# When raw weight slots are given back, and two accumulators for layer 0's modulation

## The reference, cut to what matters

```python
def modulation(cond, w_mod, b_mod):
    m = jax.nn.silu(cond) @ w_mod + b_mod
    return jnp.split(m[:, None, :], 6, axis=-1)

for li in range(DEPTH):
    sh1, sc1, g1, sh2, sc2, g2 = modulation(cond, w_mod[li], b_mod[li])
    h = x * (1 + sc1) + sh1
    ...                                   # the mixer: h @ w_in, then its own work, then @ w_out
    x = layer_norm(ALPHA * x + g1 * out, ln_g[li, 0], ln_b[li, 0])
    h = x * (1 + sc2) + sh2
    x = layer_norm(ALPHA * x + g2 * moe(h, ...), ln_g[li, 1], ln_b[li, 1])
```

## Time and profile before

| | |
|---|---|
| three runs, median | 2907.91 us (2905.69 to 2911.71) |
| the profiled execution, first to last instruction | 2919.7 us |
| TensorE busy with matmuls | 2612.8 us, 89% |
| VectorE, GpSimd, ScalarE busy | 1430.2, 797.6, 752.2 us |
| weights and all else read | 517.73 MB, 179 GB/s over the span |

### The profile page before, as it was taken

The page is one execution under the profiler, slowest core; times in us unless marked ns, Lnnn a source line. Parts: engine busy times, 40 slices in busy tenths (PEclk is TensorE's granted clock), DMA queues, the critical chain, the costliest instruction groups (busy, mean ns, idle before and its releaser), DMA issues.

```text
span 2919.7 us, 30216 instructions
## 1 busy us (share of the span) xinstructions
PE 2612.8 (89%) x11960; PEld 1918.1 (66%) x11960; DVE 1430.2 (49%) x1955; ACT 752.2 (26%) x1263; POOL 797.6 (27%) x429
## 2 busy tenths in 40 slices
PE   5779899998898998899998877789999899989997
PEld 3778864445896787744458866676444699864444
DVE  6456553334645676633336389974333415650013
ACT  1132130002454451300013344432001334230111
POOL 3355400001363344000014478830000247500000
PEclk8789889998699998899999878898999899979999
DMA  7443639893241216388944411054989143528881
GB/s 265 168 124 101 193 143 334 321 360 110 76 137 37 73 58 180 137 326 316 362 162 138 143 48 37 24 183 150 332 324 348 51 135 101 149 99 300 301 297 41
DMA packets 291851, 524.41 MB, mean 180 GB/s; under 512 B 9472, under 2 KB 141056, under 8 KB 291328
## 3 DMA queue, kind: packets, MB, share of 16 engines
q1 hardware_dynamic: 288256, 519.33, 51.4%
q10 hardware_dynamic: 3456, 3.15, 0.3%
HBM read 517.73 MB, written 4.72 MB: 179 GB/s over the span
## 4 chain that ended last, share of the span: by engine, by line
PE 75%; DVE 12%; ACT 4%; DMA 3%; issue 3%; POOL 2%; SPq 0%; ACTq 0%; DVEq 0%
PE ps L1877 23%; PE ps L1892 11%; PE ps L1625 6%; PE ps L1626 6%; PE ps L1627 6%; PE ps L1690 3%; DVE macc L1964 2%; POOL wlo L1557 2%; DVE uw L1318 2%; PE ps L1648 1%; PE ps L1816 1%; PE ps L1650 1%; PE ps L1649 1%; PE ps L1840 1%; PE ps L1841 1%
## 5 line engine op out<-in xcount | busy, mean ns | idle before, releaser
L1557 POOL TENSOR_TENSOR wlo<-ring,whi 128x1024 fp32r<-128x1024 f32 x202 | 533.6, 2657 | 1514.3 <-ACT whi L1424 1514.3
L1877 PE MATMUL ps<-ring,xg 128*128 128x512 f32 x1536 | 708.0, 606 | 0.0
L1877 PEld LDWEIGHTS ps<-ring,xg 128*128 128x128 f32 x1536 | 290.5, 194 | 329.6 <-issue 329.2
L1964 DVE SCALAR_TENSOR_TENSOR macc<-ring,cond_s,macc 128x1024 f32<-128x1024 f32 x322 | 438.9, 1424 | 10.6 <-DMA ring<-w_mod 10.6
L2182 DVE SCALAR_TENSOR_TENSOR hid<-ps,cws,sg 128x256 f32<-128x256 f32 x96 | 46.4, 484 | 674.6 <-ACT sg L1518 674.6
L1892 PE MATMUL ps<-ring,hidt 128*128 128x512 f32 x768 | 349.9, 599 | 2.3 <-ACT hidt L1493 2.3
L1625 PE MATMUL ps<-hh,whi 128*128 128x384 f32 x832 | 303.4, 365 | 27.3 <-POOL wlo L1557 21.0
L1626 PE MATMUL ps<-hl,whi 128*128 128x384 f32 x832 | 291.0, 350 | 0.0
L1627 PE MATMUL ps<-hh,wlo 128*128 128x384 f32 x832 | 290.9, 350 | 0.0
L1424 ACT ACTIVATE whi<-ring 128x1024 fp32r<-128x1024 f32 x202 | 207.2, 1055 | 307.4 <-DMA ring<-gmlp_w_out 115.2
L1892 PEld LDWEIGHTS ps<-ring,hidt 128*128 128x128 f32 x768 | 147.4, 193 | 187.4 <-issue 187.4
(11 more groups left out here) (361 smaller groups left out, 4112.3 us busy)
## 6 DMA issues: line engine op xcount, KB each, us to landing
ring<-moe_w_gu SPq DMA_DIRECT2D x192, 1024.0 KB, 7.5
ring<-w_mod SPq DMA_DIRECT2D x96, 1024.0 KB, 8.2
ring<-moe_w_down SPq DMA_DIRECT2D x96, 1024.0 KB, 5.1
ring<-gmlp_w_in SPq DMA_DIRECT2D x32, 1024.0 KB, 5.7
ring<-ssd_w_in SPq DMA_DIRECT2D x21, 1024.0 KB, 5.3
ring<-hgrn_w_in SPq DMA_DIRECT2D x20, 1024.0 KB, 5.2
ring<-gmlp_w_out SPq DMA_DIRECT2D x16, 1024.0 KB, 5.7
ring<-ssd_w_out SPq DMA_DIRECT2D x8, 1024.0 KB, 6.0
```

Of the source, the lines that this page charges most:

```text
L1557: pool.tensor_tensor(split_sub(wlo, s0), raw_sub(s0), split_sub(whi, s0).bitcast(F32), ALU.subtract).then_inc(S["lo_ready"], 1)
L1877: ins = pe.matmul(ps[:, s % 2, :], xg[:, w, k, :], whole(what, s, 4)[:, k % 4, :], start=(k == 0), stop=(k == KD - 1))
L1964: ins = dve.scalar_tensor_tensor(out=macc[:, v, :], in0=w[:, k, :], scalar=by, in1=macc[:, v, :], op0=ALU.mult, op1=ALU.add)
```

## The change

A slot that held a mixer chunk is given back when GpSimd has written the low part of its second half (`lo_ready`), and not when TensorE has finished it (`sub_done`). Raw weights are read by ScalarE and GpSimd alone, so nothing reads the slot after that. The counts in the wait are the same.

Groups 2 and 4 of layer 0 add into a second accumulator, `macc_b`, which lies where the gated MLP's `gsh` comes to lie later. The first chunk of a group waits for the sum of the last group before it that used the same accumulator and was not done by TensorE alone, in place of the group just before it. The other groups and layers stay on `macc`.

```diff
@@ -57,6 +57,7 @@
 PE_GROUPS = (1,)
+B_GROUPS = (2, 4)
@@ -242,6 +243,7 @@
         macc = ar("macc", [P, 2, D], F32, 76)
+        macc_b = ar("macc_b", [P, 2, D], F32, 24)
@@ -379,7 +381,7 @@
                 elif chunk_rows[p] > 0:
-                    sp.wait_ge(S["sub_done"], nth[2 * p] + 2)
+                    sp.wait_ge(S["lo_ready"], nth[2 * p] + 2)
@@ -513,6 +515,10 @@
+        def acc_of(group):
+
+            return macc_b if group in B_GROUPS else macc
@@ -1687,7 +1693,7 @@
-                    ins = pe.matmul(ps[:, 7, c:c + 1], macc[:, v, j * P:(j + 1) * P], ones[:, 0:1], start=True, stop=True)
+                    ins = pe.matmul(ps[:, 7, c:c + 1], acc_of(group)[:, v, j * P:(j + 1) * P], ones[:, 0:1], start=True, stop=True)
@@ -1953,15 +1959,19 @@
                 elif q == 0:
-                    dve.wait_ge(S["mod_summed"], m // MOD_GROUP)
+                    group = m // MOD_GROUP
+                    held = max((g for g in range(group) if acc_of(g) is acc_of(group) and g not in PE_GROUPS), default=None)
+                    if held is not None:
+                        dve.wait_ge(S["mod_summed"], held + 1)
+                acc = acc_of(m // MOD_GROUP)
...
-                            ins = dve.tensor_scalar(macc[:, v, :], w[:, k, :], by, None, ALU.mult)
+                            ins = dve.tensor_scalar(acc[:, v, :], w[:, k, :], by, None, ALU.mult)
...
-                            ins = dve.scalar_tensor_tensor(out=macc[:, v, :], in0=w[:, k, :], scalar=by, in1=macc[:, v, :],
+                            ins = dve.scalar_tensor_tensor(out=acc[:, v, :], in0=w[:, k, :], scalar=by, in1=acc[:, v, :],
```

## The result

The changed kernel takes 2928.6 us in the median of 12 runs (2916.7 to 2932.3), the kernel before 2910.6 us beside it; the ratio is 1.0051, with a 95% interval of 1.0038 to 1.0064. One of the 12 runs of before, in a slow state, took 3431.7 us and does not enter the ratio. I had forecast 6.1 us and a range up to 2920.5. The direction was right, the size was not. The profiled execution of the changed kernel spans 2922.9 us, only 3.2 us more than that of before: that of the changed kernel lay 4 us under its median, that of before about 11 above.

The account below looks back on a forecast made before the run. It took TensorE, three quarters of the chain that ended last, to bound the kernel. Terms of 0 + 0.4 + 4.6 + 3.2 - 2.1 = +6.1 us on 2907.9 gave 2914.0 us, range 2902.5 to 2920.5.

Parts of the forecast that it names:

- the two out-part terms: Out parts of layers 0 and 1: earlier low parts meet VectorE's modulation chunks, delaying the last out chunk; +0.4 and +4.6 us.
- The second accumulator: Layer 0's V part: VectorE's 19.40 us idle time stays, as `mod_take` of group 2 waits for the same sum; 0 us.
- Start of layer 0's out part: Out chunk 1 loads earlier, so ScalarE's 3.09 us wait for it goes; -2.85 us.
- End of layer 0's out part: Out chunk 6's low parts meet modulation chunk 5, so the last out chunk lands late; +3.25 us.
- Layer 1's out part: Low parts of out chunks 4 and 6 meet modulation chunks 3 and 5; last tile starts later, +4.6 us.
- TensorE's clock: After the new stall in each of layers 0 and 1's out parts, a lower granted clock; 2 x 1.6 = 3.2 us.
- Layer 2: F chunk 1 loads earlier, -2.7 us; in the out part the last chunk meets VectorE, +0.6; together -2.1 us.
- The Z part: High part waits for a place in `whi` after landing, so an earlier load just waits in its slot; 0 us.
- B: Rival: gains come without collision, VectorE reaching modulation chunk 5 first in layers 0 and 1; -4.95 us, 2903.0; chance 0.20.
- C: Rival: effects cancel, layer 1's sum not late (+2.4), no clock dip; +0.7 us, 2908.6; chance 0.22.
- D: Rival: VectorE's idle 19.4 us before group 3 of layer 0 shrinks; 2888 us or below; chance 0.03.
- E: Rival: each stall brings two stretches at 1.2 GHz, layer 1's late sum its own dip; +11, 2919; chance 0.13.

Follow-up runs that it names:

- e4: Kernel before with the new slot rule only for the out chunks of layers 0 and 1, one accumulator: ratio 1.0062, +18 us on before.
- e3: Changed kernel with one accumulator and the out chunks of layers 0 and 1 back on `sub_done`: ratio 0.9986, -4 us on before.
- e6: Changed kernel, but GpSimd holds low parts of out chunks 4 and 6 in layers 0 and 1 until VectorE's modulation chunks 3 and 5 are done: ratio 1.0006.
- e2: Kernel before with only the second accumulator added, slots still given back by `sub_done`: ratio 1.0000 on before.
- e1: Kernel before with the slot rule alone, all groups on one accumulator: ratio 1.0068, +19.8 us on before.
- e12: Kernel before with the new slot rule only for layer 2's out chunks, one accumulator: ratio 1.0012, +3.5 us on before.
- e9: Kernel before with the new slot rule only for layer 0's U and layer 2's Q and F chunks, one accumulator: ratio 0.9983, 2906.4 us.
- e13: Changed kernel, GpSimd holding low parts of out chunks in layers 0, 1 and 2, layer 1's XS and Z chunks back on `sub_done`: ratio 0.9992 on before.
- e15: Changed kernel, but GpSimd holds back the low parts of out chunks 4 and 6 in layer 1 alone: ratio 1.0024, +7.0 us on before.
- e11: Kernel before with the new slot rule only for layer 1's XS and Z chunks, one accumulator: ratio 1.0006 on before.
- e10: Changed kernel, but layer 0's first expert load waits for ScalarE's rounding of the last out chunk's first half; run once for its profile, no time given.

## Why the prediction was wrong in size

The step that failed is the size of the two out-part terms. With the clock I had given them 0.4 + 2.85 + 4.6 + 3.2 = 11.05 us; by themselves they measure 18 us (e4, 11.6 to 24.7). The rest of the sum held: I had -4.95 us for all other places, and the kernel without those two terms measures -4 us (e3, -8.4 to +0.3). The mechanism, low parts beside VectorE's chunk and the last pair of loads late behind it, was right (e6). Term by term:

- **The second accumulator: 0.** Right (e2; 19.08 us before L1982).
- **Start of layer 0's out part, -2.85 us.** Right in kind, -2.2 in all traces with the rule there. The load behind it did land late as before (wait of 11.35 us against 11.18).
- **End of layer 0's out part, +3.25 us for the tile.** The mechanism was right to each link; the size was not. In e4, which has no gain ahead, the tile starts 6.1 us late. Chunk 5 took 9.1 us where I had 8.5 (+0.6). The last out chunk took 9.76 us to land where I had put the 8.4 of the earlier trace rows (+1.4): a price carried from another pair. From landing to TensorE's start it took 4.6 us where I had 3.7 (+0.9): GpSimd's low part itself waited for a step of VectorE, 3.30 us. In the changed kernel chunk 5 also met a low part of out chunk 5 (11.0 us). (A slip besides: 356.6 less 2.85 is 353.75, not 353.9, so the term should have read +3.1.)
- **Layer 1's out part, +4.6 us.** Of the two this is the one that was off most: 9.6 us in the traces for 6.2 with the clock. I had the sum after tile 3 0.8 us late and let that be part of the 4.6 us. It is 1.5 us late, the stretch at 1.2 GHz at this place is 3.4 us longer for it, and TensorE is 3.7 us later from then on (e1, 1128 to 1136 us). The chain of tile 4, chunk 5 and the last loads starts from there; so the stall of 4.3 us at the last tile comes on top, with 3.6 us net of the 0.65 that e2 has, 1.5 us for the clock behind it, and 1.1 us more by 1250 us.
- **TensorE's clock, 1.6 us in each of two places.** The price was near (1.3 us in e4, 1.8 in the changed kernel and 2.7 in e1 behind layer 0's stall, 1.5 behind layer 1's last, about 2 at the late sum), the count was not: two more places, the late sum, where an old stretch grows, and layer 2's `y_t` (1.9 us with a granted clock of 0.53 behind it in e6). My upper bound was too low: in before's trace the matmuls from 2533.8 to 2537.0 us, at 1.2 GHz, start 0.32 us apart, which makes 7.7 us for a half tile of 24 and not 7.1.
- **Layer 2, -2.1 us.** The F part gave -2.5 to -2.8 as forecast. The out part cost 0 to 4 us in the traces with the rule (3.5 us in e12's runs, 0 to 7) and not 0.6: I had followed the load and not VectorE's own next duty. Its chunk of 11 us stands ahead of `y_t`, which TensorE wants for its mean. How much of this is the rule's stays open (e9).
- **The Z part, 0.** Wrong in the trace (+3.7); in time the runs can't tell it from nothing, and e3, which has it, is 4 us under before. I had looked at whether `whi` holds the high part back, and not at what the freed load queue does to a small load just ahead.
- **Rivals.** B (no collision) is what e6 and e13 make of the kernel, near zero or under it. C, which cancels, and D fell. E, +11 with a dip of its own at the late sum, was nearest and still at the lower end of what was measured, with 0.13. To slower as a whole I had given 0.47, so the direction was no firm forecast.
- The sum of my terms with the sizes of the traces put in is 18 to 20 us; the runs say 14.8 (11 to 18.6) for the changed kernel and 19.8 (13 to 26) for e1, which differs by a second accumulator that alone does nothing; the two intervals overlap.

## What to carry to other kernels

When a buffer is given back earlier, follow the transfer to its landing and look up which engine then works on it, and what else runs at that moment: here a correct earlier release put GpSimd's work beside VectorE's, and the chunk of VectorE that released the next loads took twice as long. If a chain feeds two stalls of the bound engine, the later stall adds to the earlier one; don't let one sum cover both. Take the early release only where a wait for the load is on the path (e9), or fix the order of the two engines by hand (e13).

## What the runs showed that I had not expected

- A start 0.3 us later, behind another engine's instruction and not ahead of it, made a VectorE instruction take 2.80 us for 0.69, and TensorE stand 2.06 us for it.
- Taking the meetings out of layer 1 (e6, e15), or only delaying its Z part (e3, e11), also took away a stretch at 1.2 GHz that had been there. Windows of e2 and of e6 over the same 33 matmuls, some of them overlapping the window's ends:

```profile
1130.00:1138.00 8.00, 8.00 (x33) 7.39 (x33) 5.57 (x7) 2.00 (x2) 3.46 (x2) 0.57 0.52 141
```

```profile
1128.50:1133.20 4.70, 4.70 (x33) 4.43 (x33) 3.72 (x7) 0.35 (x1) 0.43 (x1) 1.00 0.88 242
```

They take 8.0 us at a clock of 0.57 and 4.7 us at 1.00. No stall of TensorE stands directly ahead in e2; the 32 matmuls of one column of the sum do, and they do in e6 as well. What brings this stretch on I can't say.
- The second of a pair of 1 MB loads lands 8.3 to 8.6 us after its issue in some traces and 9.5 to 9.9 us in others at the same place, in one of them (e10, 9.5 us) with no third load beside it.
- Two profiled executions of equal work (before and e2) differ by 10 us in their spans, nearly all of it in a few stretches at 1.2 GHz.
